# Token mixer of a hybrid block: attention products paired over halves of the array, decay rows broadcast by the tile loads

## The chip, the cores and the metric

The kernel runs on one core of a Trainium2 chip. The core has engines that run side by side and meet at semaphores: TensorE (PE in the rows, with PEld for the loads of its stationary operand), VectorE (DVE), ScalarE (ACT), GpSimd (POOL), and SyncE (SP), which here only starts DMAs. The metric is the time of one execution in device microseconds (us); smaller is better.

## The reference

One layer of an encoder block on 1024 tokens of width 1024, all in float32. The change touches the token mixer alone:

```python
def token_mixer(x, w_in, conv_w, a_log, dt_bias, norm_w, sinks, w_out):
    proj = x @ w_in
    ...
    gdn = gated_deltanet(qkv, z, b_raw, a_raw, conv_w, a_log, dt_bias, norm_w)
    swa = sliding_window_sink_attention(sq, sk, sv, sinks)
    return jnp.concatenate([gdn, swa], axis=-1) @ w_out
# gated_deltanet: 4 heads of 128, per chunk
    gam = cumsum(g);  decay = exp(gam_i - gam_j)
    a_mat = beta * strict_decay * (k @ k.T);  qk = (q @ k.T) * decay
    solve (I + a_mat) u = beta * v - beta * exp(gam) * k @ state
    o = q * exp(gam) @ state + qk @ u;  state = exp(gam_end) * state + k_dec.T @ u
# sliding_window_sink_attention: 8 query heads of 64, 2 key heads, window of 128
    s = q @ k.T / 8;  m = max(max(s), sink);  p = exp(s - m)
    p = p / (sum(p) + exp(sink - m));  o = p @ v
```

After it come a layer norm (x1), the PEER feed-forward (product-key retrieval over 16384 experts, 8 heads, top 16), and a second layer norm. Most of the kernel's time lies there, and the change leaves it as it is.

## The kernel before

`build` runs stages one after another: `project` (the input projection, to about 302 us), `mix_tokens` (the mixer, to about 785 us), then `split_x1`, `retrieve`, `index_picks`, `build_gates` and `experts`. A stage begins when all engines have left the one before.

`mix_tokens` works through 8 tiles of 128 tokens. Each engine has its own program, in an order written out by hand; the semaphores in `S` tie them together. A tile's work on PE, in `body(c, i, s, before, after)`:

- transposes of k and v (L594, L596), and the attention scores of half the heads (`scores(s, 0)`, L536: four products with 64 rows of contraction and 256 columns; the first call uses rows 0 to 63 of the array, `scores(s, 1)` rows 64 to 127);
- six levels (LV = 6, n = 0 to 5) that invert the triangular matrix by doubling. A level is L613 (the product x), then filler, then a wait for VectorE's masked copy `xs` (L923, semaphore `lm`), then L633 (skipped in the last level) and L636. VectorE adds their results to `tu[0]` (L930, semaphore `la`) and `tu[1]` (L938, semaphore `lb`);
- the filler in a level: a share (2, 2, 2, 2, 3, 3 and, after the levels, 2) of the output projection of the tile before (`project_out`, L530, three products of 512 columns for each share), the transposes of the probabilities of heads 0 to 3 (n = 2, L543), the scores of the other half (n = 3), and the steps of `ahead`, which prepare the next tile's decay matrices;
- after the levels: L642, L651 (the solution u, copied by ScalarE in L770), L657, L659, L660, the transposes of the other probabilities (L543), the values (L672: 16 products, pT stationary, 64 columns of v moving), the transposes of og (L677) and of the attention output on (L681). ScalarE copies the two results into `mixT` hi (L782, L784), VectorE takes the low parts (L989). The next tile's scores wait for the low part of the attention half, its projection for both.

`ahead` for tile d: VectorE spreads the decay sums over 128 columns (gB, L839), adds the causal mask to the keys' part (e0, L841), PE turns gB into rows that stand on every partition, four products for the k part (L552) and four for the q part (L557), both into PSUM bank 1; VectorE adds e0 to each (L845, L848, into `dm`), ScalarE takes the exponentials (eg, L738, and dm, L740). The products of keys with keys (L563) and with queries (L569) follow in the same bank, and VectorE multiplies them by dm (L855, L858).

The softmax of a half: VectorE scales and masks the scores (`softmax_scores`, L871), takes the maxima (`softmax_max`, L879 to L884), ScalarE the exponentials (L720, four calls of 128x256 with their sums, and L723), PE transposes, ScalarE copies to pT (`evacuate_probs`, L727). The division by the sum is done on the output (L968, L970, L981).

SP loads each tile's operands (`load`, five DMAs on L462, and `load_x`) for two tiles at the start, later for tile c + 2 as soon as tile c has released them. The w_out rows come in eight loads (L487), which tile 0 splits into high and low parts.

## Time and profile before

| | us |
|---|---|
| runs: median of 3 (lowest, highest) | 3359.24 (3352.19, 3367.15) |
| the profiled execution | 3360.03 |
| its span in the trace | 3358.4 |
| PE busy over the span | 2814.9 |
| VectorE busy | 2310.0 |
| ScalarE busy | 932.6 |
| GpSimd busy | 1587.4 |

The time is the span and 1.6 us around it. Stages do not overlap, so a microsecond that the mixer's last engine gains or loses is one of the kernel's time. A busy share over the whole span says nothing of a stage; the mixer's own rows are below. The profile's chain of waits begins at 1609 us and says nothing of the mixer, so its chain is followed in the instructions in order of time.

### The profile page before, as it was taken

To read this page: it belongs to the slowest core of one execution; us is meant where nothing else is said; L and a number is where in the kernel's file an instruction comes from. 1 tells how busy PE (TensorE), PEld (TensorE's weight loads), DVE (VectorE), ACT (ScalarE), POOL (GpSimd) and SP (SyncE) were. 2 spreads that over 40 slices of the span, in tenths; PEclk is the share of its full clock that TensorE was granted. 3 is DMA by queue.
4 is the path that set the end of the run, shared out by engine and by line. 5 is a ranking of instruction groups with operands and counts; after the bars stand their busy time and mean duration, and the time that the engine had idled before them with its cause. 6 is when DMAs were issued, how large, how long until landed. Compare 5 with 4: busy or idle time off the path is not lost.

```text
span 3358.4 us, 39617 instructions
## 1 busy us (share of the span) xinstructions
PE 2814.9 (84%) x14408; PEld 2187.2 (65%) x14408; DVE 2310.0 (69%) x4936; ACT 932.6 (28%) x1295; POOL 1587.4 (47%) x1196
## 2 busy tenths in 40 slices
PE   7996799996988546564466999999999999999996
PEld 6896788885766446553244667676667776766664
DVE  4511666651899989996576777777877777775445
ACT  4311322321444434342111222222222222222221
POOL 0000000101577755553666664666665667653543
PEclk9987899997988777877788999999999999999998
DMA  3323211202211059998999998999999999997984
GB/s 129 106 71 97 71 44 56 66 13 102 71 48 35 32 180 305 302 303 232 404 393 387 388 390 328 397 394 386 377 385 342 401 381 391 391 355 280 343 331 175
DMA packets 383433, 829.65 MB, mean 247 GB/s; under 512 B 158080, under 2 KB 180992, under 8 KB 383264
## 3 DMA queue, kind: packets, MB, share of 16 engines
q0 software_dynamic: 150864, 548.60, 42.7%
q1 hardware_dynamic: 232400, 278.84, 24.8%
q8 instruction: 100, 1.64, 0.2%
q14 instruction: 69, 0.57, 0.0%
HBM read 768.49 MB, written 58.85 MB: 246 GB/s over the span
## 4 chain that ended last, share of the span: by engine, by line
PE 15%; DMA 13%; POOL 12%; DVE 8%; issue 4%; ACT 0%; POOLq 0%; DVEq 0%; ACTq 0%
DMA e_u_row<-in_u,id_u 11%; POOL hold L1775 8%; POOL e_u_row L1766 4%; DVE e_u_row L1979 3%; PE psum L1837 3%; PE psum L1802 2%; PE psum L1823 2%; PE psum L1803 2%; PE psum L1804 2%; PE psum L1824 2%; PE psum L1825 2%; DMA hold<-in_v,id_v 2%; DVE e_y L1970 1%; DVE e_ul L1937 1%; DVE e_vl L1941 1%
## 5 line engine op out<-in xcount | busy, mean ns | idle before, releaser
L1775 POOL DMA_INDIRECT hold<-in_v,id_v x512 | 577.3, 1128 | 316.2 <-PE psum L1837 172.8
L1979 DVE CUSTOM_DVE_ANT_0 e_u_row<-e_u_row,hold 128x1024 f32<-128x1024 f32 x384 | 467.9, 1223 | 280.7 <-DMA e_u_row<-in_u,id_u 249.9
L1766 POOL DMA_INDIRECT e_u_row<-in_u,id_u x384 | 482.9, 1257 | 372.5 <-DVE hidden_s L1979 241.3
L1823 PE MATMUL psum<-e_vh,e_ah 128*128 128x512 f32 x1024 | 425.1, 415 | 114.2 <-DVE e_y L1970 83.1
L1824 PE MATMUL psum<-e_vl,e_ah 128*128 128x512 f32 x1024 | 412.3, 403 | 0.0
L1825 PE MATMUL psum<-e_vh,e_al 128*128 128x512 f32 x1024 | 410.1, 400 | 0.0
L1970 DVE TENSOR_TENSOR e_y<-e_y,psum 128x512 f32<-128x512 f32 x504 | 327.7, 681 | 82.7 <-PE psum L1825 57.3
L1823 PEld LDWEIGHTS psum<-e_vh,e_ah 128*128 128x128 f32 x1024 | 199.9, 195 | 230.3 <-DVE e_y L1970 103.3
L1802 PE MATMUL psum<-x1d_hi,e_uh 128*128 128x512 f32 x864 | 342.7, 397 | 0.0
L1803 PE MATMUL psum<-x1d_lo,e_uh 128*128 128x512 f32 x864 | 337.5, 391 | 0.0
L1804 PE MATMUL psum<-x1d_hi,e_ul 128*128 128x512 f32 x864 | 336.4, 389 | 0.0
L1533 PE MATMUL psum<-g_one,g_two 128*128 128x128 f32 x1024 | 176.9, 353 | 148.6 <-issue 133.2
L1837 PE MATMUL psum<-hold,e_column 128*32 128x512 f32 x2048 | 249.5, 605 | 34.3 <-DMA hold<-in_v,id_v 27.5
L1533 PEld LDWEIGHTS psum<-g_one,g_two 128*128 128x128 f32 x1024 | 171.8, 266 | 161.5 <-issue 161.5
L1588 POOL DMA_INDIRECT hold<-in_u,id_u x128 | 197.7, 1544 | 165.0 <-DVE hidden_s L1562 135.0
L1882 ACT ACTIVATE e_a<-psum 128x512 f32<-128x512 f32 x108 | 64.4, 596 | 621.7 <-PE psum L1804 456.2
L1004 POOL TENSOR_TENSOR m_h<-m_h,m_lng 128x1024 f32<-128x1024 f32 x8 | 18.8, 2352 | 451.1 <-DVE m_h L905 451.1
L1825 PEld LDWEIGHTS psum<-e_vh,e_al 128*128 128x128 f32 x1024 | 199.7, 195 | 45.0
L1824 PEld LDWEIGHTS psum<-e_vl,e_ah 128*128 128x128 f32 x1024 | 200.8, 196 | 39.5
L1871 ACT ACTIVATE e_vh<-e_vr 128x1024 fp32r<-128x1024 f32 x128 | 135.2, 1056 | 302.2 <-DMA e_vr<-in_v 276.1
L1802 PEld LDWEIGHTS psum<-x1d_hi,e_uh 128*128 128x128 f32 x864 | 162.1, 188 | 75.0 <-issue 41.9
L1603 ACT ACTIVATE g_tile<-psum 128x512 f32<-128x512 f32 x128 | 131.6, 1089 | 216.8 <-PE psum L1533 213.6
(319 smaller groups left out, 5534.0 us busy)
## 6 DMA issues: line engine op xcount, KB each, us to landing
e_vr<-in_v SPq DMA_DIRECT2D x128, 512.0 KB
e_ur<-in_uT SPq DMA_DIRECT2D x108, 512.0 KB
s_G<-g_tile SPq DMA_DIRECT2D x8, 4096.0 KB, 29.6
e_g<-s_G SPq DMA_DIRECT2D x128, 256.0 KB
p_wr<-in_w_ch SPq DMA_DIRECT2D x17, 512.0 KB, 3.8
s_ch<-p_out POOLq DMA_DIRECT2D x16, 512.0 KB, 3.8
m_ch<-s_ch SPq DMA_DIRECT2D x8, 1024.0 KB, 5.9
r_w<-in_wq SPq DMA_DIRECT2D x16, 512.0 KB
```

What stands on the lines that cost most here:

```text
L1533: last = nc.tensor.matmul(psum[:, n // 4, (n % 4) * NK:(n % 4 + 1) * NK], one2[s][:, n, :], one1[s][:, n, :], start=True, stop=True)
L1766: pool.indirect_dma_start(out=u_ring[n % U_RING][:], out_offset=None, in_=io["u"], in_offset=bass.IndirectOffsetOnAxis(ap=id_u[:, s, k:k + ...
L1775: pool.indirect_dma_start(out=v_ring[m % V_RING], out_offset=None, in_=io["v"], in_offset=bass.IndirectOffsetOnAxis(ap=id_v[:, t:t + 1], a ...
L1802: nc.tensor.matmul(psum[:, j, :], uh[j][:, k, :], x1d[0][:, k, :], start=(k == 0), stop=False)
L1803: nc.tensor.matmul(psum[:, j, :], uh[j][:, k, :], x1d[1][:, k, :], start=False, stop=False)
L1804: last = nc.tensor.matmul(psum[:, j, :], ul[j][:, k, :], x1d[0][:, k, :], start=False, stop=(k == KC - 1))
L1823: nc.tensor.matmul(acc, ah[s][j][:, r], vh[s][j][:, c], start=(j == 0), stop=False)
L1824: nc.tensor.matmul(acc, ah[s][j][:, r], vl[s][j][:, c], start=False, stop=False)
L1825: last = nc.tensor.matmul(acc, al[s][j][:, r], vh[s][j][:, c], start=False, stop=(j == 1))
L1837: last = nc.tensor.matmul(psum[32 * j:32 * j + 32, 6 + c, :], column[:, 32 * (4 * (n % Z_RING) + j) + 31 - i:32 * (4 * (n % Z_RING) + j) + ...
L1970: add = nc.vector.tensor_tensor(y[:, t, c], y[:, t, c], psum[:, 2 + q % 4, :], ALU.add)
L1979: nc.vector.tensor_tensor_reduce(row, row, xs[:, s, :], 1.0, 0.0, ALU.mult, ALU.add, hs[:, s, k:k + 1]).then_inc(dotted, 1)
```

## The change

Three parts, joined:

1. **Decay rows by DMA.** The sums of all tiles are transposed once (64x128), copied to `rowT`, stored to a tensor in HBM, and each tile's rows are loaded broadcast over 128 partitions (`rowB`, 512 KB a tile). gB, L552 and L557 go. VectorE and ScalarE read the rows from SBUF.
2. **Scores with alternating row halves.** A half of the heads is now two query blocks times both key heads: the four products of a call alternate between rows 0 to 63 (to PSUM bank 4) and rows 64 to 127 (to bank 5). The host reorders the sinks and the rows of w_out to match.
3. **Stationary values.** v (64 columns) is stationary and pT (128 columns) moves; the two key heads go to column halves 0 and 64 of the array. The output comes out transposed, so L681, `on` and its copy go. Since the queries now lie along the columns, the probabilities are divided beforehand: ScalarE scales each head's 128x256 (`scale_probs`, four calls a half, semaphore `p_nrm`), for which VectorE adds and inverts the sums a half at a time (`softmax_sum`).

Around these: the first transposes of probabilities move from n = 2 to n = 3, the second scores from n = 3 to n = 4, the second maxima from n = 4 to n = 5, and at the tile's end the attention half of `mixT` goes first.

```diff
+                sp.wait_ge(prep["rowT"], 1)
+                sp.dma_start(scr["rows"].rearrange("c (n t) -> (c n) t", t=P), rowT[:]).then_inc(prep["stored"], 16)
+                sp.wait_ge(prep["stored"], 16)
+                for s in range(2):
+                    load_rows(sp, s, s)
                 for k in range(KC):
...
                     load(sp, c + 2, s)
+                    load_rows(sp, c + 2, s)
...
                 def scores(s, half):
-                    for n in range(4):
-                        last = nc.tensor.matmul(ATT[:, n * 2 * P:(n + 1) * 2 * P],
-                                                ch[s][64 * half:64 * half + 64, N_CONV + n, :],
-                                                kw[s][64 * half:64 * half + 64, :], start=True, stop=True)
+                    for m in range(2):
+                        for r in range(2):
+                            rows_r = slice(AD * r, AD * r + AD)
+                            last = nc.tensor.matmul(psum[:, 4 + r, m * 2 * P:(m + 1) * 2 * P],
+                                                    ch[s][rows_r, N_CONV + 2 * half + m, :],
+                                                    kw[s][rows_r, :], start=True, stop=True)
...
-                        if n == 2:
-                            pe.wait_ge(S["prob"], 2 * c + 1)
+                        if n == 3:
+                            pe.wait_ge(S["p_nrm"], 2 * c + 1)
                             transpose_probs(0)
-                        if n == 3:
+                        if n == 4:
                             pe.wait_ge(S["p_ev"], 2 * c + 1)
                             scores(s, 1)
-                        if after and n in (0, 1, 2, 4):
-                            ahead(c + 1, i + s, 1 - s, min(n, 3))
+                        if after and n in (2, 4):
+                            ahead(c + 1, i + s, 1 - s, 2 if n == 2 else 3)
...
-                    for a in range(AH):
-                        r = a // 4
+                    for p in range(4):
                         for k in range(2):
-                            last = nc.tensor.matmul(psum[:, 4, a * AD:(a + 1) * AD], pT[:, a, k, :],
-                                                    vw[s][:, k, r * AD:(r + 1) * AD], start=(k == 0), stop=(k == 1))
+                            for r in range(2):
+                                last = nc.tensor.matmul(psum[AD * r:AD * r + AD, 4, p * P:(p + 1) * P],
+                                                        vw[s][:, k, AD * r:AD * r + AD],
+                                                        pT[:, 4 * (p // 2) + 2 * r + p % 2, k, :], start=(k == 0), stop=(k == 1),
+                                                        tile_position=(0, AD * r))
...
+                def scale_probs(c, half):
+                    act.wait_ge(S["rec"], 2 * c + half + 1)
+                    for a in range(4 * half, 4 * half + 4):
+                        last = nc.scalar.activation(sc[:, a, :], sc[:, a, :], ACT.Copy, scale=mx[:, 3, a:a + 1])
+                    last.then_inc(S["p_nrm"], 1)
...
                     nc.scalar.activation(uu[:], bank(1), ACT.Copy).then_inc(S["u_ev"], 1)
+                    scale_probs(c, 1)
                     act.wait_ge(S["ods"], now)
...
-                        dve.wait_ge(S["row_a"], d + 1)
+                        dve.wait_ge(tile_in[s][6], 16 * (i + 1))
                         dve.wait_ge(S["e0"], d + 1)
-                        nc.vector.tensor_tensor(dm[:, 0], bank(1), e_heads, ALU.add).then_inc(S["add_a"], 1)
+                        nc.vector.tensor_tensor(dm[:, 0], rowB[s][:, 0], e_heads, ALU.add).then_inc(S["add_a"], 1)
```

Where the instructions stand, on three places. PE at the end of a tile and the beginning of the next one (m_pT holds the transposed probabilities, m_vw the values). Before:

```order
L584 MATMUL psum<-cst,m_tu 128x128 x4
L672 MATMUL psum<-m_vw,m_pT 128x64 x16
L677 MATMUL psum<-cst,m_og 128x128 x4
L681 MATMUL psum<-cst,m_on 128x128 x4
L594 MATMUL psum<-cst,m_ch 128x128 x4
L596 MATMUL psum<-cst,m_ch 128x128 x4
L536 MATMUL psum<-m_kw,m_ch 128x256 x4
L613 MATMUL psum<-m_tu,m_aq 128x128 x4
```

After:

```order
L588 MATMUL psum<-cst,m_tu 128x128 x4
L676 MATMUL psum<-m_pT,m_vw 64x128 x16
L683 MATMUL psum<-cst,m_og 128x128 x4
L598 MATMUL psum<-cst,m_ch 128x128 x4
L600 MATMUL psum<-cst,m_ch 128x128 x4
L551 MATMUL psum<-m_kw,m_ch 128x256 x4
L617 MATMUL psum<-m_tu,m_aq 128x128 x4
```

The values have changed their operands, and the transposes of m_on are gone.

VectorE in levels 0 and 1 of tile 0 (later tiles have the same order). Before:

```order
L923 TENSOR_TENSOR m_xs<-psum,mats 128x512
L839 COPY m_gB<-m_rows 128x1024
L841 TENSOR_TENSOR m_e<-mats,m_nkey 128x512
L930 TENSOR_TENSOR m_tu<-m_tu,psum 128x512
L938 TENSOR_TENSOR m_tu<-m_tu,psum 128x512
L879 TENSOR_REDUCE m_mx<-m_sc 128x4
L881 TENSOR_TENSOR m_mx<-m_mx,m_sinks 128x4
L883 TENSOR_TENSOR m_mx<-m_sinks,m_mx 128x4
L884 TENSOR_SCALAR m_mx<-m_mx 128x4
L845 TENSOR_TENSOR m_dm<-psum,m_e 128x512
L923 TENSOR_TENSOR m_xs<-psum,mats 128x512
```

After:

```order
L939 TENSOR_TENSOR m_xs<-psum,mats 128x512
L849 TENSOR_TENSOR m_e<-mats,m_nkey 128x512
L946 TENSOR_TENSOR m_tu<-m_tu,psum 128x512
L953 TENSOR_TENSOR m_tu<-m_tu,psum 128x512
L887 TENSOR_REDUCE m_mx<-m_sc 128x4
L889 TENSOR_TENSOR m_mx<-m_mx,m_sinks 128x4
L891 TENSOR_TENSOR m_mx<-m_sinks,m_mx 128x4
L892 TENSOR_SCALAR m_mx<-m_mx 128x4
L853 TENSOR_TENSOR m_dm<-m_rowB,m_e 128x512
L939 TENSOR_TENSOR m_xs<-psum,mats 128x512
```

Only the copy to m_gB is gone; what stands between the add to m_tu and the next m_xs is the same.

VectorE in levels 4 and 5 of tile 0 (m_wout_lo is split in tile 0 alone; later tiles have the rest in this order). Before:

```order
L923 TENSOR_TENSOR m_xs<-psum,mats 128x512
L930 TENSOR_TENSOR m_tu<-m_tu,psum 128x512
L879 TENSOR_REDUCE m_mx<-m_sc 128x4
L881 TENSOR_TENSOR m_mx<-m_mx,m_sinks 128x4
L883 TENSOR_TENSOR m_mx<-m_sinks,m_mx 128x4
L884 TENSOR_SCALAR m_mx<-m_mx 128x4
L938 TENSOR_TENSOR m_tu<-m_tu,psum 128x512
L858 TENSOR_TENSOR m_aq<-psum,m_dm 128x512
L910 TENSOR_TENSOR m_wout_lo<-m_wout_raw,m_wout_hi 128x1024
L923 TENSOR_TENSOR m_xs<-psum,mats 128x512
L935 TENSOR_TENSOR m_faded<-m_state,m_decay 128x512
L938 TENSOR_TENSOR m_tu<-m_tu,psum 128x512
```

After:

```order
L946 TENSOR_TENSOR m_tu<-m_tu,psum 128x512
L953 TENSOR_TENSOR m_tu<-m_tu,psum 128x512
L879 SCALAR_TENSOR_TENSOR m_sc<-psum,m_wm 128x1024
L866 TENSOR_TENSOR m_aq<-psum,m_dm 128x512
L926 TENSOR_TENSOR m_wout_lo<-m_wout_raw,m_wout_hi 128x1024
L939 TENSOR_TENSOR m_xs<-psum,mats 128x512
L887 TENSOR_REDUCE m_mx<-m_sc 128x4
L889 TENSOR_TENSOR m_mx<-m_mx,m_sinks 128x4
L891 TENSOR_TENSOR m_mx<-m_sinks,m_mx 128x4
L892 TENSOR_SCALAR m_mx<-m_mx 128x4
L950 TENSOR_TENSOR m_faded<-m_state,m_decay 128x512
L953 TENSOR_TENSOR m_tu<-m_tu,psum 128x512
```

The second scores (L871, now L879) came from level 3 to level 4, and the second maxima from level 4 to the last level, behind its m_xs.

## Rows read from the trace of the kernel before

**Rows 1.** Busy time by stretch: us, busy (x) per engine, granted clock, DMA share, GB/s

```profile
333.00:385.00 52.00, 35.25 (x219) 31.62 (x219) 32.05 (x47) 15.40 (x30) 0.00 (x0) 0.83 0.25 80
...
500.00:552.30 52.30, 49.08 (x344) 42.96 (x344) 33.72 (x61) 14.03 (x32) 4.73 (x2) 1.00 0.17 53
```

**Rows 2.** Order of time, tile 3, levels 0 and 1: start, us, engine, line [idle before]

```profile
504.36 1.16 PE L613 MATMUL psum<-m_tu,m_aq 128*128 128x128 f32 x8
...
507.94 1.06 PE L633 MATMUL psum<-m_xs,m_tu 128*128 128x128 f32 x8
...
510.53 1.21 DVE L879 TENSOR_REDUCE m_mx<-m_sc 128x4 f32<-128x1024 f32 x1
...
512.75 0.68 DVE L923 TENSOR_TENSOR m_xs<-psum,mats 128x512 f32<-128x512 f32 x1
512.76 0.49 ACT L720 ACTIVATE m_sc<-m_sc,m_mx 128x256 f32<-128x256 f32 x1
...
513.88 1.06 PE L633 MATMUL psum<-m_xs,m_tu 128*128 128x128 f32 x8
```

**Rows 3.** Order of time, tile 3, levels 1 to 5 and L651

```profile
515.72 1.16 PE L613 MATMUL psum<-m_tu,m_aq 128*128 128x128 f32 x8
...
518.10 1.03 PE L543 MATMUL psum<-cst,m_sc 128*128 128x128 f32 x8
...
518.97 1.06 PE L563 MATMUL psum<-m_ch 128*128 128x128 f32 x8
...
519.87 1.06 PE L633 MATMUL psum<-m_xs,m_tu 128*128 128x128 f32 x8
...
524.19 1.99 PE L536 MATMUL psum<-m_kw,m_ch 64*128 64x256 f32 x8
...
526.11 1.16 PE L633 MATMUL psum<-m_xs,m_tu 128*128 128x128 f32 x8
...
531.99 1.06 PE L633 MATMUL psum<-m_xs,m_tu 128*128 128x128 f32 x8
...
537.22 1.16 PE L636 MATMUL psum<-m_tu,m_xs 128*128 128x128 f32 x8 [0.16 <-DVE m_xs L923]
...
541.06 1.13 PE L651 MATMUL psum<-m_vb,m_tu 128*128 128x128 f32 x8 [0.40 <-DVE m_vb L951]
```

**Rows 4.** Order of time, end of tile 3 and beginning of tile 4

```profile
547.81 3.79 PE L672 MATMUL psum<-m_vw,m_pT 128*128 128x64 f32 x32 [0.68 <-ACT m_pT L727]
...
549.61 1.13 DVE L976 SCALAR_TENSOR_TENSOR m_og<-psum,m_rms,m_zw 128x128 f32<-128x128 f32 x4
...
551.43 0.61 PE L677 MATMUL psum<-cst,m_og 128*128 128x128 f32 x4
...
554.65 1.96 PE L536 MATMUL psum<-m_kw,m_ch 64*128 64x256 f32 x8 [0.68 <-DVE m_mixT_lo L989]
...
556.54 0.97 PEld L613 LDWEIGHTS psum<-m_tu,m_aq 128*128 128x128 f32 x8 [0.33 <-issue]
```

**Rows 5.** Order of time, experts stage: eight products on four column quarters in turn

```profile
1757.55 1.92 PE L1837 MATMUL psum<-hold,e_column 128*32 128x512 f32 x16 [0.64 <-DMA hold<-in_v,id_v]
```

**Rows 6.** Order of time, tile 7, which has no step of ahead, levels 0 and 1

```profile
715.48 1.05 PE L633 MATMUL psum<-m_xs,m_tu 128*128 128x128 f32 x8
...
720.40 1.16 PE L633 MATMUL psum<-m_xs,m_tu 128*128 128x128 f32 x8 [0.54 <-DVE m_xs L923]
```

**Rows 7.** Order of time, the mixer's start (SPq: DMA issues of SP)

```profile
316.03 63.26 SPq L487 DMA_DIRECT2D m_wout_raw<-in_w_out  x8
...
317.89 0.69 DVE L845 TENSOR_TENSOR m_dm<-psum,m_e 128x512 f32<-128x512 f32 x1 [1.63 <-PE psum L552]
```

**Rows 8.** DMA issues of the page: KB each, us from issue to landing

```profile
p_wr<-in_w_ch SPq DMA_DIRECT2D x17, 512.0 KB, 3.8
```

**Rows 9.** Busy time by stretch, the mixer's start, columns as in Rows 1

```profile
306.00:322.00 16.00, 5.19 (x20) 4.49 (x20) 5.09 (x20) 6.21 (x14) 0.00 (x0) 0.50 1.05 326
```

**Rows 10.** Busy time by stretch, the projection stage, columns as in Rows 1

```profile
0.00:100.00 100.00, 81.70 (x342) 65.41 (x343) 46.72 (x43) 46.13 (x44) 4.72 (x12) 1.00 0.38 129
```

95 lines of the change are left out of this document (45 added, 50 removed).

## Prediction

> **What bounds the kernel now.** The stages do not overlap, and only the mixer changes. I read the busy times by stretch first: in one whole tile PE is busy for 49.1 of 52.3 us at the full granted clock (1.00, which is the 2.4 GHz level), VectorE for 33.7, ScalarE for 14.0 [rows 1]. So PE bounds a steady tile, but with little margin in places: the instructions in order of time show where PE waits for VectorE's m_xs or m_vb [rows 2, 3]. Then I followed tile 3 from its L613 of level 0 to that of tile 4, 504.36 to 556.54, 52.18 us [rows 2, 4]. The same order holds in tiles 1 to 6. Since every group's cost on PE follows from differences of start times, I lay the new order out with them.
>
> Costs on PE, by differences of starts. L633 and L636 together hold it for 1.84 (513.88 to 515.72), L613 and a projection share of two for 2.38 (to 518.10), the eight transposes for 0.87 (to 518.97), a group of four products such as L563 for 0.90 (to 519.87) [rows 2, 3]. Level 3 to 4 has L633, L636, L613, a share of three and L569: 5.88 less 1.84 and 0.90 leaves 3.1 for L613 with a share of three. Level 2 to 3 has L633, L636, L613, a share of two and the scores: 6.24 less 1.84 and 2.38 leaves 2.02 for a call of scores [rows 3]. Of that 0.33 is the idle time at its end [rows 4], so 1.7 is the stream of its 8 passes of 256 columns, 0.21 each. The values take 3.6 (L672 at 547.81, L677 at 551.43) [rows 4]. On VectorE an instruction over 512 columns takes 0.68 (m_xs, L923) and follows its forerunner at 0.6, or at 0.7 where it needs its result; over 1024 columns it takes 1.21 (L879) [rows 2], and I use that for the scores' mask too.
>
> **The sum for a steady tile, place by place (start of one named instruction to the next).**
>
> Level 0 (L613 to L633). Before 3.58 [rows 2]. PE no longer has L552, which leaves 2.38. But VectorE's order is vb, the scores' mask (1.2), m_xs (0.68), and since the scores come earlier (below) it is the late one: m_xs ends at about +2.6. Now 2.63.
>
> Level 0 to 1 (L633 to L633). Before 5.94 (507.94 to 513.88) [rows 2]. L557 leaves, 0.89. VectorE, though, runs without a gap from the add to m_tu through the maxima and the dm add (from 510.53, 1.6 + 0.6 us) to m_xs (512.75, ends 513.43). That stays, so PE waits: m_xs is ready at +5.5. Now 5.55, a gain of 0.4 only. Tile 7 bears this out: without any step of ahead its interval is 4.92 and PE waited 0.54 for m_xs [rows 6]; one add of 0.6 more makes 5.5.
>
> Level 1 to 2. Before 5.99 (to 519.87) [rows 2, 3]. The transposes leave for the next level, L563 stays: 1.84 + 2.38 + 0.90 = 5.1. VectorE (two m_tu adds, dm add, the new small softmax_sum of 0.4, m_xs) ends at +4.25: covered.
>
> Level 2 to 3. Before 6.24 (to 526.11) [rows 3]. The scores leave, the transposes come: 1.84 + 2.38 + 0.87 = 5.1. The transposes now wait for scale_probs. ScalarE does eg, dm, then four scalings. A call of 128x256 took 0.49 with its sum [rows 2]; at 0.5 each they end about 2.8 us before PE asks. Cost nothing; if one took 1.2 instead, the cover is gone.
>
> Level 3 to 4. Before 5.88 (to 531.99) [rows 3]. The scores come in: 1.84 + 3.1 + scores + 0.90. The price of the scores is unknown, as no row shows two row halves in turn. **Bounds:** 2.02 if they do not overlap, 1.17 if the stream of 1.7 halves. The nearest row is L1837: eight float32 products of 512 columns, two passes each, on four column quarters in turn, took 1.92 us [rows 5]. By the scores' 0.21 us for a pass of 256 columns, 16 passes of 512 would need 6.8 in a row, so 3.5 ran side by side. I take 1.17. Now 7.0; at the other end 7.85.
>
> Level 4 to 5 (L633 to L636). Before 5.23 [rows 3]. On VectorE the mask of the scores (1.2) replaces the maxima (1.6); the path m_tu, mask, aq, m_xs ends at +5.1. Now 5.15; PE alone would need 4.9.
>
> L636 to L651. Before 3.84 [rows 3]. The maxima (1.6) now stand behind the last m_xs, before faded, m_tu, m_xs, m_vb. VectorE becomes late: 1.65 + 0.6 + 0.7 + 0.7 + 0.75 gives 4.4. A loss of 0.55. Queued behind on VectorE are softmax_sum (0.4), the layer norm and the next inverse, which have over 1 us of cover.
>
> L651 to the values. Before 6.75 (541.06 to 547.81) [rows 3, 4]. ScalarE gets four scalings, 2.0 us, in its 3.0 us of idle before og. Unchanged.
>
> Values to the next L613. Before 8.73 (547.81 to 556.54) [rows 4]. The values on two column halves: 3.6 if they do not overlap, 1.8 if they do; L1837 is the same kind of overlap and I take 1.8. The transposes of og then wait for VectorE: og ends at 550.74 [rows 4], so they run at 550.8 (0.44), and those of the next tile to 552.2. ScalarE copies the attention half at 550.1; VectorE finishes normalize (1024 columns and a reciprocal, 1.0) at 551.8 and its low part at 552.45, so the scores start at 552.55 and L613 at 553.6. Now 5.8: a gain of 2.9, of which only 0.3 hangs on the values' overlap.
>
> Sum: 2.63 + 5.55 + 5.1 + 5.1 + 7.0 + 5.15 + 4.4 + 6.75 + 5.8 = 47.5, against 52.2. **4.7 us a tile, times six: 28.2.** PE gives up L552 and L557 (1.8), the transposes of m_on (0.4), 1.7 of scores and 1.8 of values, 5.7 of work a tile; it also loses some waits, and gains others for VectorE.
>
> **Edges.** Tile 0's end gains like the others, 2.8. Tile 7: scores 0.85, end 2.9, less 0.55: 3.2. Tile 0's levels run at a granted clock of 0.83 and with waits for w_out [rows 1]; they gain at least the 2 us of a steady tile's levels, at most about 6; I take 3. The start costs: the rows must go to HBM and back. SP is free for the store at 316.0 [rows 7], while its queue of some 4.3 MB at 326 GB/s drains until about 319.5 [rows 9]. So stored at 320.3, and a 512 KB load takes 3.8 to land [rows 8]: rows at 324.4, while the first dm add ran at 317.89 [rows 7]. But L552, L557, L563 and the waits between them are gone from this chain: counted back from the end of the second aq at 327.9 through aq, four slow products, aq, exp and two adds, rows at 321.8 would lose nothing. Loss 3 (bounds 0 and 8). w_out's loads start 8 us later under a cover of 25. Tile 0's levels and the start cancel. In later tiles the 512 KB are asked for a whole tile ahead, at a DMA share of 0.17 [rows 1]: nothing.
>
> Total 28.2 + 2.8 + 3.2 = 34. The profiled execution took 3360.0, the median was 0.8 less: **3326 us.**
>
> The trace shows 0.33 us of idle on PE behind the scores, at the change to the full array [rows 4]. The Trainium skill, page TensorEngine Tiling (Array Packing), section Key Properties, says that a change of tiling mode drains TensorE; it speaks against the change, which puts two more such changes around the values of each tile. By that, 2 x 0.33 x 8 = 5 us more, 3331; by the rows both lie in waits that exist anyway (0.68 for m_pT ahead, 1.0 for og behind), and nothing is added. The same section says that tiles load and multiply in parallel; L1837 agrees for columns (3.5 of 4), and no row shows it for row halves.
>
> **Rivals.**
> *The row halves do not overlap.* For it: nothing shows it, and both halves give to the same columns of the array. Level 3 to 4 loses 0.85, level 0 only 0.45, since VectorE is late there. 1.3 x 6 + 1.7 = 9.5: 3335. If the values do not overlap either, 0.3 x 8 more: 3338.
> *Waits on VectorE or ScalarE eat half the gain.* Three places are already set by VectorE, and I counted semaphore hops tightly; 0.3 us more at each of nine places is 2.7 a tile: 3342 to 3347.
> *Slower: the clock falls.* PE's busy share drops from 94% to about 90%, with waits of 1.4 us in level 1 and 1.1 before L651. Tile 0 shows what it costs: busy 68%, clock 0.83 [rows 1]. At 0.83 the 43 us of PE work a tile would need 8.9 more, 62 in seven tiles: 3388. It decides from a mean clock under 0.89. Against it: the projection stage is busy 82% at 1.00 [rows 10].
> *More gain than counted:* tile 0 at 6 instead of 3, the start free: 3320, and with less idle between places 3315.
>
> **How the numbers follow.** Forecast (3319 to 3332) 0.54; row halves serial (3333 to 3339) 0.20; half the gain eaten (3340 to 3350) 0.12; more than counted (3308 to 3318) 0.09; clock or an unknown stall (over 3350) 0.05. A measurement can tell about 0.5%, 16.8 us, from no change, so faster means under 3342.4: all of the first, second and fourth and a part of the third, 0.86; same 0.11; slower 0.03 (the clock's case, which lies above 3376 only if it holds in most tiles). The range 3312 to 3344 leaves out half of the fourth case, most of the fifth and part of the third, and takes in both ends of the scores' price and of the start.
>
> **What would show it.** A tile's period of about 47 us; L617 of level 0 to L637 under 2.8; level 0 to 1 at 5.5 with PE waiting 1.4 for m_xs; the scores' group at 1.2 and the values' at 1.8; no wait of PE for ScalarE's m_sc at the transposes; granted clock 1.00 from tile 1 on; the first dm add at 324 to 325. Wrong if the clock is under 1 in tiles 1 to 6, if the scores take 2.0, or if scale_probs ends late.

## The result, and the profile after

| | us |
|---|---|
| changed kernel, median of 4 runs (lowest, highest) | 3315.69 (3315.04, 3317.66) |
| kernel before, median of 4 runs on the same chip | 3361.89 (3352.19, 3367.15) |
| ratio, 95% interval | 0.9859 (0.9843, 0.9875) |
| the profiled execution, its span | 3315.04, 3313.4 |
| PE, VectorE, ScalarE busy | 2766.4, 2303.7, 957.6 |

The change saves 46 us by the two medians, where 34 were forecast. (The median before moved by 2.7 us, from 3359.24 to 3361.89, when a fourth run came to it; against the forecast of 3326 the changed kernel is 10 us lower.) The first question is where in the program they were saved. The mixer ends where SP issues the first load of `t_x`: at 786.70 before, at 745.76 now, 40.9 us earlier. The remaining 4.1 us of the two profiled executions lie in later stages that the change doesn't touch; they turn out to be within chance (see the second run of this kernel below).

The order of time on PE in tile 3 of the changed kernel, which answers to [rows 2 to 4], without the projection's products: start, us, engine, line, shape, and in brackets the idle time before and what ended it.

```profile
486.85 1.16 PE L617 MATMUL psum<-m_tu,m_aq 128*128 128x128 f32 x8
...
489.44 1.16 PE L637 MATMUL psum<-m_xs,m_tu 128*128 128x128 f32 x8
...
495.25 1.16 PE L637 MATMUL psum<-m_xs,m_tu 128*128 128x128 f32 x8 [1.32 <-DVE m_xs L939]
...
500.47 1.06 PE L637 MATMUL psum<-m_xs,m_tu 128*128 128x128 f32 x8
...
504.69 1.03 PE L558 MATMUL psum<-cst,m_sc 128*128 128x128 f32 x8
505.56 1.06 PE L637 MATMUL psum<-m_xs,m_tu 128*128 128x128 f32 x8
...
510.54 1.14 PE L551 MATMUL psum<-m_kw,m_ch 64*128 64x256 f32 x8
511.60 1.16 PE L573 MATMUL psum<-m_ch 128*128 128x128 f32 x8
512.60 1.06 PE L637 MATMUL psum<-m_xs,m_tu 128*128 128x128 f32 x8
...
517.66 1.16 PE L640 MATMUL psum<-m_tu,m_xs 128*128 128x128 f32 x8
...
521.96 1.13 PE L655 MATMUL psum<-m_vb,m_tu 128*128 128x128 f32 x8 [0.86 <-DVE m_vb L968]
...
528.71 1.97 PE L676 MATMUL psum<-m_pT,m_vw 128*64 128x128 f32 x32 [0.68 <-ACT m_pT L736]
531.70 0.66 PE L683 MATMUL psum<-cst,m_og 128*128 128x128 f32 x4 [1.02 <-DVE m_og L991]
...
533.30 1.14 PE L551 MATMUL psum<-m_kw,m_ch 64*128 64x256 f32 x8
```

Read it by differences of starts, as the sum was made. The scores hold PE from 510.54 to L573 at 511.60, 1.06 us, where a call took 1.92 to 2.02 before [rows 3, 4]. The values take 1.97 instead of 3.79 (by the length of the row; counted to the next group's start they took about 3.6 before). Each transpose of the probabilities comes without a wait. The next tile's L617 starts at 534.37, so this tile took 47.52 us against 52.18; the six steady tiles average 47.41. The last columns of the next view (busy time by stretch: us, busy and count of PE, PEld, VectorE, ScalarE and GpSimd, granted clock, DMA share, GB/s) answer to [rows 1].

```profile
338.00:374.00 36.00, 24.50 (x183) 21.88 (x182) 28.80 (x47) 14.54 (x31) 0.00 (x0) 0.93 0.22 67
427.00:474.50 47.50, 43.09 (x324) 37.53 (x324) 33.10 (x61) 16.95 (x39) 4.75 (x2) 1.00 0.21 70
...
522.00:569.50 47.50, 43.31 (x326) 37.72 (x327) 33.30 (x62) 16.96 (x39) 4.76 (x2) 1.00 0.21 69
```

PE is busy 91% of a steady tile instead of 94%, and the granted clock stays at 1.00. The start of the mixer answers to [rows 7]:

```profile
316.22 0.55 SPq L489 DMA_DIRECT2D s_rows<-m_rowT  x1
...
321.36 0.80 SPq L465 DMA_DIRECT2D m_rowB<-s_rows  x2
...
325.26 0.69 DVE L853 TENSOR_TENSOR m_dm<-m_rowB,m_e 128x512 f32<-128x512 f32 x1 [7.36 <-DMA m_rowB<-s_rows]
```

The rows went to HBM in 5.1 us and back in 3.9, and the first dm addition started at 325.26 instead of 317.89. VectorE idled 7.36 us for it, but level 0 of tile 0 began only 2.57 us later (338.45, before 335.88).

### The profile page after: what moved, and what is told of

It is laid out like the page before. It is cut to its first block, busy times and chain, and to the rows that moved or that the text cites. A ratio compares the mean times of both kernels' runs of the same rounds, so it can differ in the third digit from the quotient of the medians.

```text
span 3313.4 us, 39366 instructions
## 1 busy us (share of the span) xinstructions
PE 2766.4 (83%) x14249; PEld 2138.5 (65%) x14249; DVE 2303.7 (70%) x4936; ACT 957.6 (29%) x1360; POOL 1582.5 (48%) x1196
## 4 chain that ended last, share of the span: by engine, by line
PE 18%; DMA 13%; POOL 9%; DVE 9%; issue 4%; ACT 0%; POOLq 0%; DVEq 0%
DMA e_u_row<-in_u,id_u 12%; POOL hold L1785 6%; DVE e_u_row L1989 4%; PE psum L1847 3%; POOL e_u_row L1776 3%; PE psum L1833 3%; PE psum L1812 3%; PE psum L1813 2%; PE psum L1814 2%; PE psum L1834 2%; PE psum L1835 2%; DVE e_y L1980 1%; DVE e_ul L1947 1%; DVE e_al L1967 1%; DVE e_vl L1951 1%
## 5 line engine op out<-in xcount | busy, mean ns | idle before, releaser
L1847 PE MATMUL psum<-hold,e_column 128*32 128x512 f32 x2048 | 250.1, 607 | 28.6 <-DMA hold<-in_v,id_v 22.8
```

The source lines that it names most:

```text
L1847: last = nc.tensor.matmul(psum[32 * j:32 * j + 32, 6 + c, :], column[:, 32 * (4 * (n % Z_RING) + j) + 31 - i:32 * (4 * (n % Z_RING) + j) + ...
```

## The experiments

Each is compared by the first `t_x` issue of its profiled execution, which leaves the later stages out. Where an execution started the mixer late (the load of `m_alog` was issued at 303.8 before, and between 302.1 and 305.4 in the others), the text says so and takes it off. "A tile" is the mean of the six steady ones.

### Each part alone

The broadcast of the rows alone, on the kernel before (attention, softmax and levels as before):

```diff
-                        nc.vector.tensor_tensor(dm[:, 0], bank(1), e_heads, ALU.add).then_inc(S["add_a"], 1)
+                        nc.vector.tensor_tensor(dm[:, 0], rowB[s][:, 0], e_heads, ALU.add).then_inc(S["add_a"], 1)
...
+                    load_rows(sp, c + 2, s)
```

> The kernel before with part 1 alone (decay rows by DMA; scores, values and the order of levels as before). If the steady-tile sum holds: level 0 loses L552 and its wait (1.1 us), level 0 to 1 only 0.4 since VectorE sets it, so 1.5 a tile in seven tiles, less 2.6 at the start: about 8 us less than before, 3353 to 3355. Rival, every product removed counts in full: 1.8 a tile, less 2.6: 3351. Rival, the round trip through HBM and the loads cost more than they give: 3362 or more.

Measured: 3353.96 us, the median of 10 runs (3345.58 to 3365.46), ratio 0.9977 (0.9964 to 0.9991). Its first `t_x` issue is at 781.1, 7.2 earlier than before once the 1.6 us of a later start are off. A tile takes 51.14 on the mean, but one of the six is an outlier: the end of tile 6 ran for a while at the lower level of TensorE's clock (of the row of busy times below, as in [rows 1], the third number from the right is the granted clock).

```profile
702.00:706.00 4.00, 4.00 (x19) 3.60 (x20) 2.27 (x5) 1.30 (x3) 0.93 (x1) 0.50 0.02 4
```

That tile took 52.71 us; the other five average 50.83, a gain of 1.35. The time of 3354 is what the steady-tile sum said, and the 1.35 is near its 1.5.

The attention alone, that is the changed kernel with gB, L552 and L557 back:

```diff
-                        nc.vector.tensor_tensor(dm[:, 0], rowB[s][:, 0], e_heads, ALU.add).then_inc(S["add_a"], 1)
+                        nc.vector.tensor_tensor(dm[:, 0], bank(1), e_heads, ALU.add).then_inc(S["add_a"], 1)
...
-                    load_rows(sp, c + 2, s)
```

> The changed kernel without part 1 (gB and its products on PE are back), so parts 2 and 3 and the shifted levels alone. If the parts add up: about 8 us more than the changed kernel, 3324, that is 38 less than before. Rival, the parts need each other (VectorE's copy to m_gB eats the room that the shorter scores made): 3330 or more.

Measured: 3326.93 us (3324.80 to 3332.26), ratio 0.9891 (0.9871 to 0.9912); first `t_x` issue 756.7, a tile 49.57. The time lies between the 3324 of parts that add up and the 3330 of parts that need each other.

The ratios of the parts multiply to 0.9868, within the interval of the whole. By the tile, though, the parts give 1.35 (without the outlier) and 2.61 us, 3.96 together, and the change gives 4.77. The missing 0.8 has a place. From L613 of level 0 to that of level 1 the kernel before took 5.42 us, the rows alone 4.21, the attention alone 6.63, both 4.53 or 4.31. With the attention alone, PE reaches the filler of level 0 sooner, and VectorE's chain that ends in gB is late:

```profile
490.01 1.16 PE L614 MATMUL psum<-m_tu,m_aq 128*128 128x128 f32 x8
...
493.81 1.16 PE L553 MATMUL psum<-cst,m_gB 128*128 128x128 f32 x8 [1.25 <-DVE m_gB L845]
```

```profile
492.47 1.28 DVE L845 COPY m_gB<-m_rows 128x1024 f32 x1
493.67 0.68 DVE L847 TENSOR_TENSOR m_e<-mats,m_nkey 128x512 f32<-128x512 f32 x1
```

These are rows of the attention alone, tile 3, first of PE and then of VectorE. PE stands 1.25 us in front of L553 until the copy of gB (492.47, 1.28 us) is done. The other part removes this copy. So each part is worth more when the other is there.

### Is it the order of the halves that shortens the scores?

The four products of a call in the order half, product instead of product, half. Two of one row half then stand in a row:

```diff
-                    for m in range(2):
-                        for r in range(2):
+                    for r in range(2):
+                        for m in range(2):
```

> The changed kernel with the four products of a call of scores in the order rows 0 to 63 twice, then rows 64 to 127 twice, instead of alternating. If the alternating halves overlap on the array: the group goes from 1.06 us back to about 1.9, levels 3 to 4 lose 0.85 a tile, level 0 about 0.4: 3325. Rival, the group is short for another reason (the banks, or loads that run ahead): 3316 and a group of 1.1.

Measured: 3318.19 us (3316.76 to 3320.68), ratio 0.9868 (0.9847 to 0.9889); first `t_x` issue 745.7, a tile 47.40. What I held to be needed, the alternation, is not. The scores of this kernel, level 4 of tile 3:

```profile
512.13 1.14 PE L551 MATMUL psum<-m_kw,m_ch 64*128 64x256 f32 x8
513.20 1.16 PE L573 MATMUL psum<-m_ch 128*128 128x128 f32 x8
```

1.07 us, as in the change. That left two explanations: two row halves overlap without being alternated, or the group is short for another reason, such as the two banks of the accumulator. The next kernel tells them apart. It keeps the change's order and banks but takes all four products from row half 0, so half of the scores are those of other heads:

```diff
-                            rows_r = slice(AD * r, AD * r + AD)
+                            rows_r = slice(0, AD)
```

> The changed kernel with all four products of a group of scores in row half 0 (stationary and moving both from partitions 0 to 63), written to banks 4 and 5 in the same alternation as in the change; so half of the scores are of other heads than they should be, and everything after them is the same work on other numbers. If two row halves working at once is what shortens the group, it is back at 1.9 to 2.1 us a group (passes one by one every 0.215 us), 0.9 us longer, twice a tile on TensorE's path: a tile of 49.1 to 49.3, the first t_x issue 759 to 761 instead of 745.76, 3329 to 3332. If the alternation of two banks of the accumulator is what shortens it, the group stays at 1.06 us, the tile at 47.4, the first t_x issue at 745 to 747.

Measured: 3334.04 us in one run; first `t_x` issue 763.4, a tile 48.92. The scores of level 4, tile 3:

```profile
521.16 1.99 PE L551 MATMUL psum<-m_kw,m_ch 64*128 64x256 f32 x8
523.08 1.16 PE L573 MATMUL psum<-m_ch 128*128 128x128 f32 x8
```

1.92 us, as before the change. So two row halves at work at once shorten the scores, and the alternation of banks by itself does not. Whether the two halves would still overlap if both wrote to one bank, no run shows. Its price per tile was 1.5 us, less than the 1.7 to 1.9 expected. The issue at 763.4 is above the 759 to 761 expected, and the time above its 3329 to 3332, since tile 0 began 2.1 us later and took 59.04 us against 53.36. The lower clock is a part of both. This is the granted clock around the start of tile 0, in this kernel and then in the change:

```profile
334.00:342.00 8.00, 7.94 (x27) 6.40 (x28) 2.52 (x4) 0.60 (x1) 0.00 (x0) 0.50 0.00 0
342.00:350.00 8.00, 6.09 (x27) 5.50 (x26) 4.71 (x9) 0.47 (x2) 0.00 (x0) 0.56 0.00 0
```

```profile
334.00:342.00 8.00, 7.16 (x41) 6.03 (x42) 4.06 (x6) 0.60 (x1) 0.00 (x0) 0.74 0.00 0
342.00:350.00 8.00, 5.47 (x45) 5.00 (x43) 6.23 (x14) 4.14 (x12) 0.00 (x0) 1.00 0.01 2
```

The first scores took 3.78 us there (1.87 in the change), and level 0 to 1 took 6.43 (3.94). So what this one run says of row halves is read from the steady tiles.

### The same question for the values

First all eight products of one column half and then those of the other:

```diff
-                    for p in range(4):
-                        for k in range(2):
-                            for r in range(2):
+                    for r in range(2):
+                        for p in range(4):
+                            for k in range(2):
```

> The changed kernel with all values of the first key head (column half 0) before those of the second, so that neighbours on PE use the same half. If halves overlap only when they alternate: the group goes from 1.9 us to about 3.5, but only 0.3 a tile shows, since the wait for m_og (1.0 us idle before L683) covers the rest: 3318. Rival, all of it shows: 1.6 in eight tiles, 3329.

Measured: 3319.54 us (3314.53 to 3328.22), ratio 0.9866 (0.9843 to 0.9889); first `t_x` issue 747.7, a tile 47.65. Then two of one half in a row, and two of the other:

```diff
                     for p in range(4):
-                        for k in range(2):
-                            for r in range(2):
+                        for r in range(2):
+                            for k in range(2):
```

> The changed kernel with the 16 products of the values in the order pair, half, block: two products of one column half in a row, then two of the other, instead of turn by turn. With eight in a row the group took 3.33 us instead of 1.97 and no passes overlapped. If TensorE looks a few instructions ahead and starts the other half's product while this half's is still running, two in a row overlap as the four scores did: 1.9 to 2.2 us. If column halves overlap only where the program alternates them: 3.2 to 3.5 us, or, where only each change of half overlaps, 2.5 to 2.9. In each case the tile is little changed (the og transposes wait for VectorE then anyway): the first t_x issue 745 to 748.

Measured: 3327.74 us in one run; first `t_x` issue 749.6, of which 1.6 are a later start, a tile 47.39. (The expectation for the column halves and the one for the tile both held. The time of this single run is high through stages behind the mixer, see below.) The values in tile 3, first of the eight in a row, then of the pairs:

```profile
531.10 3.33 PE L676 MATMUL psum<-m_pT,m_vw 128*64 128x128 f32 x32 [0.68 <-ACT m_pT L736]
534.36 0.66 PE L683 MATMUL psum<-cst,m_og 128*128 128x128 f32 x4
```

```profile
531.41 2.02 PE L676 MATMUL psum<-m_pT,m_vw 128*64 128x128 f32 x32 [0.68 <-ACT m_pT L736]
534.39 0.66 PE L683 MATMUL psum<-cst,m_og 128*128 128x128 f32 x4 [0.97 <-DVE m_og L991]
```

Eight in a row take 3.33 us, two in a row 2.02, turn by turn 1.97. How far apart two halves may stand is in the same trace. The trace has two passes for each float32 product, 32 for the group. Cut at two moments, the eight in a row of tile 3 are

```profile
531.10 1.63 PE L676 MATMUL psum<-m_pT,m_vw 128*64 128x128 f32 x13 [0.68 <-ACT m_pT L736]
531.10 2.02 PE L676 MATMUL psum<-m_pT,m_vw 128*64 128x128 f32 x20 [0.68 <-ACT m_pT L736]
```

Thirteen passes have started by 532.465, seven more by 532.85, and the last twelve by 534.16. Pass by pass, the starts lie 0.11 us apart (only the first gap is 0.16) up to the twelfth and from the 21st on, and in between two such series run side by side: the last four passes of the one half with the first four of the other. All eight tiles have this pattern. So in this group PE brings the other half forward by four passes, two products, and not more, which is what both kernels with two of one half in a row need. (The trace doesn't name the half of a pass; that is read from the two series.) And the 1.36 us that eight in a row cost the group cost the tile only 0.24: before L683, PE waits for VectorE's `m_og` anyway (1.02 idle in the change, 0.97 with the pairs, none with eight in a row). That is the cover that the prediction put at all but 0.3.

No kernel separates the rest of part 3. From the values to the next L617 a steady tile gained 3.07 us (8.73 to 5.66), the largest gain of all places. With the scores in one row half this interval is 6.49, so 0.8 of it are the next tile's scores; the other 2.2 belong to the stationary values, the transposes that went with them and the attention half of `mixT` going first, together.

### Tile 0: what the shift by a level is worth

The largest miss was tile 0's levels: 7.2 us gained where 3 were put. I took the parts of the change alone there, and one more kernel, the kernel before with nothing but the shift (transposes in level 3, second scores in level 4, their mask and maxima one level later):

```diff
-                        if n == 2:
+                        if n == 3:
                             pe.wait_ge(S["prob"], 2 * c + 1)
                             transpose_probs(0)
-                        if n == 3:
+                        if n == 4:
                             pe.wait_ge(S["p_ev"], 2 * c + 1)
                             scores(s, 1)
```

> The kernel before with only the level shift of the attention: transposes of the first probabilities in level 3 instead of 2, second scores and their mask and maxima one level later. Nothing else of the change. What is measured is how much of tile 0's 7.2 us comes from the shift. My theory: in tile 0 the second scores stood at level 3 behind a pT copy that ScalarE made late, among the copies of w_out (PE idle 1.68 us there at 356.85), and the shift takes that wait away: L613 to L651 of tile 0 goes from 41.97 us to 37 to 39, steady tiles (52.17 us each) move by no more than 0.3, the first t_x issue comes at 781 to 786 instead of 786.70, and the time is 3355 to 3362. Rival 1: the shift by itself does nothing in tile 0 (41 to 42 us there), and the 5.4 us that the attention part gave tile 0 came from shorter groups and fewer instructions: no change, 3360 to 3364. Rival 2: the shift also carries much of the steady gain: a tile of 51.2 or less, the first t_x issue by 778, 3352 or less.

Measured: 3361.75 us, the median of 10 runs (3353.77 to 3371.90), ratio 1.0001 (0.9985 to 1.0017); first `t_x` issue 785.1, of which 1.6 are a later start, a tile 52.47. In the time the shift by itself makes no difference that can be measured: in the trace, tile 0 gains 3.3 us and each steady tile loses 0.3, both as expected. Tile 0 of five kernels, from one level's start to the next, in us:

| tile 0 | before | shift | rows | attention | both (after) |
|---|---|---|---|---|---|
| level 0 to 1 | 5.42 | 5.42 | 3.92 | 5.44 | 3.94 |
| level 1 to 2 | 7.50 | 7.49 | 6.20 | 5.92 | 5.63 |
| level 2 to 3 | 5.21 | 5.22 | 5.51 | 5.42 | 5.43 |
| level 3 to 4 | 8.25 | 5.16 | 9.11 | 5.17 | 5.17 |
| level 4 to 5 | 5.75 | 5.85 | 5.79 | 4.98 | 4.99 |
| level 5 to the u product | 9.84 | 9.67 | 8.93 | 9.68 | 9.61 |
| sum | 41.97 | 38.81 | 39.46 | 36.61 | 34.77 |

3.1 of the 7.2 us are the shift's, all between levels 3 and 4; 3.35 come from levels 0 to 2; 0.8 from the shorter scores in level 4. What stood there, tile 0 of the kernel before:

```profile
338.47 1.16 PE L552 MATMUL psum<-cst,m_gB 128*128 128x128 f32 x8 [1.43 <-DVE m_gB L839]
...
344.39 1.67 PE L557 MATMUL psum<-cst,m_gB 128*128 128x128 f32 x8 [1.93 <-DVE m_dm L845]
...
356.85 2.18 PE L536 MATMUL psum<-m_kw,m_ch 64*128 64x256 f32 x8 [1.68 <-ACT m_pT L727]
358.97 2.08 PE L633 MATMUL psum<-m_xs,m_tu 128*128 128x128 f32 x8
...
366.07 1.16 PE L633 MATMUL psum<-m_xs,m_tu 128*128 128x128 f32 x8 [1.86 <-DVE m_xs L923]
```

It is tempting to read the gain off these waits, but others stand in their places. The same two levels of the changed kernel, 1 and 3:

```profile
346.08 1.16 PE L637 MATMUL psum<-m_xs,m_tu 128*128 128x128 f32 x8 [2.53 <-DVE m_xs L939]
...
356.68 1.16 PE L637 MATMUL psum<-m_xs,m_tu 128*128 128x128 f32 x8 [1.19 <-DVE m_xs L939]
```

Over levels 0 to 4, PE's waits fall only from 7.4 to 6.0 us. The larger part is what PE has to do and how fast. L552 and L557 are gone, which held PE for 0.99 and 1.46 us. The second scores, 2.1 us, stood in level 3 behind ScalarE's copy to pT, which came late among the copies of w_out; one level later the copy is long done, and the scores fill time in which PE waited 1.86 for `m_xs`. And the kernel before ran twice at the lower of the clock's two levels (granted clock 0.62 and 0.69, as a mean of the stretch):

```profile
344.50:349.00 4.50, 4.50 (x26) 4.50 (x27) 1.12 (x3) 2.87 (x9) 0.00 (x0) 0.62 0.02 4
...
356.50:362.00 5.50, 5.15 (x22) 4.45 (x23) 1.38 (x3) 1.36 (x2) 0.00 (x0) 0.69 0.30 95
```

L633 and L636 took 2.95 us in the first (345.85 to 348.80) and 3.29 in the second (358.97 to 362.26), where 1.84 is usual: 2.6 us in all. In the changed kernel the granted clock is 1.00 from 342 to 360. Level 1 to 2 of the attention alone shows how much this is: it has L557's counterpart and the same wait of 1.93 ahead of it, its clock stays at 1.00, and it takes 5.92 us instead of 7.50. Why the clock fell in one kernel and not in the other, no run shows: PE's wait in level 1 alone doesn't decide it, since the change waits 2.53 us there and stays at 1.00. With the shift alone the first slow stretch is still there and the second is gone.

### VectorE's order, and tile 0 once more

After the change PE waits for VectorE at two places of a tile, 1.32 us in level 1 and 0.86 ahead of L655. In this kernel the dm addition of the k part goes from level 0 to level 1, the second mask ahead of the m_tu update of level 4, the second maxima to the end of level 4, and the second aq product from level 4 to level 5:

```diff
+                        if n == 4:
+                            softmax_scores(c, s, 1)
                         if n < LV - 1:
...
                         if n == 5:
-                            softmax_max(c, 1)
+                            if after:
+                                ahead(c + 1, i + s, 1 - s, 5)
...
                         if n == 4:
-                            softmax_scores(c, s, 1)
-                        if after and n in (0, 1, 2, 4):
-                            ahead(c + 1, i + s, 1 - s, {0: 1, 1: 2, 2: 4, 4: 5}[n])
+                            softmax_max(c, 1)
+                        if after and n == 1:
+                            ahead(c + 1, i + s, 1 - s, 1)
+                        if after and n in (1, 2):
+                            ahead(c + 1, i + s, 1 - s, {1: 2, 2: 4}[n])
```

> The changed kernel with VectorE's work in another order: the first dm addition for the next tile at level 1 instead of 0, the second mask ahead of the update of tu in level 4, the second maxima at the end of level 4, the second aq product after the mask of level 5. No work is added or left out. My theory: after the change TensorE waits for VectorE at two places of each tile, 1.32 us for m_xs in level 1 and 0.86 us for m_vb ahead of the u product; with these additions out of the way both shrink, 1.2 to 1.9 us less a tile of 47.4, the first t_x issue 10 to 15 us before 745.76, the time 3301 to 3306. Rival: the wait goes from one level to the next, since VectorE's whole work of a tile is what sets these levels: a tile of 47.0 to 47.6, the time 3312 to 3318. Second rival: the moved additions delay the masks or tu in level 1 or 5, which are waited for at once: a tile over 47.8, 3319 or more.

Measured: 3310.14 us (3307.66 to 3320.21), ratio 0.9843 (0.9825 to 0.9862); first `t_x` issue 739.7. A tile takes 46.08, 1.33 less, within what was expected. The waits of tile 3:

```profile
495.32 1.16 PE L637 MATMUL psum<-m_xs,m_tu 128*128 128x128 f32 x8 [0.62 <-DVE m_xs L939]
...
521.48 1.13 PE L655 MATMUL psum<-m_vb,m_tu 128*128 128x128 f32 x8 [0.40 <-DVE m_vb L973]
```

But the time lies between the two cases expected (3301 to 3306, or 3312 to 3318), and the mixer gained only 6 us of the expected 10 to 15, since tile 0 took 57.05 us instead of 53.36. To see whether that was the order's doing or chance, the changed kernel itself ran again beside three others on one chip:

> The changed kernel itself once more, unchanged, for two numbers: how much its time varies, and whether the 4.1 us that its profiled run gained behind the mixer (from the first t_x issue to the end 2567.6 us, before 2571.7) belong to it. In the other eight kernels of this study the same unchanged stages took 2569.0 to 2578.9 us. If they vary by chance: this run's stretch lies anywhere in 2567 to 2579 us, the first t_x issue at 745 to 747, and the median of its runs at 3315 to 3321. If the change makes them faster: 2567 to 2568 again, and a median of 3314 to 3317.

Measured: 3321.74 us, the median of 4 runs (3314.98 to 3328.16), ratio 0.9878 (0.9854 to 0.9903); first `t_x` issue 746.7. Its levels are as in the first profile, but its tile 0 took 56.00 us. The place, on PE in the first profile, on PE in this one, and on ScalarE in this one:

```profile
379.60 2.08 PE L661 MATMUL psum<-m_uu,m_kd 128*128 128x128 f32 x8 [3.45 <-ACT m_uu L780]
```

```profile
381.47 2.08 PE L661 MATMUL psum<-m_uu,m_kd 128*128 128x128 f32 x8 [5.38 <-ACT m_uu L780]
```

```profile
379.88 1.06 ACT L757 ACTIVATE m_wout_hi<-m_wout_raw 128x1024 fp32r<-128x1024 f32 x1 [2.52 <-DMA m_wout_raw<-in_w_out]
380.84 0.58 ACT L780 ACTIVATE m_uu<-psum 128x512 f32<-128x512 f32 x1
```

PE waits for ScalarE's copy of uu, ScalarE's copy stands behind the last copy of w_out, and that waits for its load. So the end of tile 0 hangs on how long a load takes, and the same kernel differs by 2.6 us there: 1.9 in this wait and the rest in the products behind it, which ran at the lower clock for longer. Tile 7 varies too, in the other direction: from its values to the first `t_x` issue the first profile has 31.19 us and this one 29.58. Behind the mixer this execution took 2571.0 us, the first one 2567.6, the kernel before 2571.7. Over the fourteen executions profiled here that stretch lies between 2567.2 and 2578.9. So the 4.1 us behind the mixer are well within what chance does.

The next kernel takes that wait away: ScalarE's last two copies of w_out stand behind its copy of uu.

```diff
                         split_wout(5)
-                        split_wout(6)
-                        split_wout(7)
                     act.wait_ge(S["u_mm"], now)
                     nc.scalar.activation(uu[:], bank(1), ACT.Copy).then_inc(S["u_ev"], 1)
+                    if not before:
+                        split_wout(6)
                     scale_probs(c, 1)
+                    if not before:
+                        split_wout(7)
```

> The changed kernel with ScalarE's last two copies of w_out in tile 0 put behind its copy of uu (all other order unchanged). In tile 0 the copy of uu came at 378.97 because a w_out copy ahead of it waited for its load, while the u product had been ready about 3.6 us earlier. If the w_out copies are what is left of tile 0's excess: u product to values in tile 0 falls from 12.7 us to 8.5 to 9.5, and the first t_x issue comes at 741 to 743. Rival: the clock stays at 1.2 GHz longer, or VectorE's splitting of the last two blocks is late instead, and 1 us or less is left: 744.5 to 746.

Measured: 3312.26 us in one run; first `t_x` issue 743.4, of which 1.4 are a later start. From the u product to the values tile 0 takes 9.12 us instead of 12.71 and 15.36: the u product at 374.60 and the copy of uu right behind it.

```profile
376.71 0.60 ACT L778 ACTIVATE m_uu<-psum 128x512 f32<-128x512 f32 x1 [2.67 <-PE psum L655]
...
383.72 1.97 PE L676 MATMUL psum<-m_pT,m_vw 128*64 128x128 f32 x32 [0.68 <-ACT m_pT L736]
```

VectorE's order in tiles 1 to 7 only, with the change's order in tile 0 (`if before` at each moved instruction):

> The changed kernel with the order of the run vector_order on VectorE in tiles 1 to 7 alone, and its own order in tile 0. There a tile fell from 47.41 to 46.08 us, but tile 0 grew by 3.6 us. If tile 0's loss came from the order of its instructions among the w_out copies: the first t_x issue at 736.5 to 738.5 (745.76 less 6 times 1.33 and what tile 7 gives), 3306 to 3310. If it came from the clock, by chance of the run: 739 to 742, 3309 to 3313.

Measured: 3314.20 us (3307.64 to 3314.79), ratio 0.9848 (0.9828 to 0.9868); first `t_x` issue 740.5, of which 1.5 are a later start; a tile 46.08, tile 0 54.54. The issue, also without the later start (739.0), lies in the second case of the expectation (739 to 742), if at its edge; the time is above both cases (3306 to 3313). The rows still find a part for the first case. Of tile 0's 3.7 us with the order in every tile, 1.5 stood ahead of the u product (36.25 us against 34.77), and they are gone here (34.75). In the eight profiled executions that have the change's order in tile 0 up to there and scores on both halves, this one among them, the sum is 34.75 to 34.77, so the 1.5 belong to the order. They came by way of the clock: with VectorE's order in tile 0, L637 and L640 of level 1 took 3.46 us (345.41 to 348.87) where 1.84 is usual. The rest stood at the w_out load, where even one and the same kernel differs by 2.6, and can't be told from chance.

Both edits together:

> The two edits together: VectorE's order in tiles 1 to 7 and ScalarE's last two w_out copies behind the copy of uu. If they add up: the first t_x issue at 733 to 735, the time 3302 to 3308, some 12 us below the changed kernel and the fastest of this study. Rival: tile 0's gain is lost again at the start of tile 1, where the projection waits for VectorE's last w_out block: as vector_order_from_1 within 1 us.

Measured: 3307.46 us (3304.01 to 3309.99), ratio 0.9837 (0.9818 to 0.9855); first `t_x` issue 730.6, or 732.4 without its earlier start; tile 0 48.39, a tile 46.08. They add up. This is the fastest kernel of the study, 14 us below the changed kernel's four runs on the same chip and 8 below its first four.

## Why the prediction was right, and which term was off

The forecast was 3326 with a range of 3312 to 3344. The changed kernel's two medians are 3315.7 and 3321.7; both lie in it. The second is in the likeliest case (3319 to 3332); the first is 3 us below it, where the case "more gain than counted" stood (3308 to 3318), which names tile 0 at 6 instead of 3. The sum, place by place, in tile 3:

| place | before | predicted | measured |
|---|---|---|---|
| level 0 (L617 to L637) | 3.58 | 2.63 | 2.59 |
| level 0 to 1 | 5.94 | 5.55 | 5.81 |
| level 1 to 2 | 5.99 | 5.1 | 5.22 |
| level 2 to 3 | 6.24 | 5.1 | 5.09 |
| level 3 to 4 | 5.88 | 7.0 | 7.04 |
| level 4 to 5 | 5.23 | 5.15 | 5.06 |
| L640 to L655 | 3.84 | 4.4 | 4.30 |
| L655 to the values | 6.75 | 6.75 | 6.75 |
| values to the next L617 | 8.73 | 5.8 | 5.66 |

Six steady tiles gave 28.6 where 28.2 were put. That holds for the waits too: PE was to wait 1.4 for `m_xs` in level 1 and did for 1.32, and scale_probs, on which the transposes wait, was early. Tile 3 on ScalarE:

```profile
499.63 1.69 ACT L731 ACTIVATE m_sc<-m_sc,m_mx 128x256 f32<-128x256 f32 x4
```

The four scalings took 1.69 us instead of 2.0 and ended at 501.3, 3.4 before L558 at 504.69, where 2.8 were put.

**The price of the scores** was bounded by 1.17 and 2.02 and taken at 1.17, by the row of eight products on column quarters [rows 5]. The group took 1.06, and the kernel with one row half puts it back at 1.92. Counted as the sum counts it (level 3 to 4 less everything else in it) the price is 7.04 - 1.84 - 3.1 - 0.90 = 1.2, so the 1.17 was right for the sum. The rival with row halves in series is dead, and the bound it stood on was the right one: that kernel lost 1.5 a tile, where 1.3 was put. What I had wrong is the cause I named in testing it: that the halves must alternate.

**The change of tiling mode.** The Trainium skill, page TensorEngine Tiling (Array Packing), section Key Properties, says that such a change drains TensorE, and 5 us were put against it as a rival. The loads of the stationary operand show it around the scores (PEld, level 4 of tile 3):

```profile
510.54 0.73 PEld L551 LDWEIGHTS psum<-m_kw,m_ch 64*128 64x128 f32 x8 [0.35 <-issue]
511.60 0.97 PEld L573 LDWEIGHTS psum<-m_ch 128*128 128x128 f32 x8 [0.33 <-issue]
```

0.35 ahead and 0.33 behind, with nothing waited for; the kernel before has 0.37 and 0.33 there. So these rows agree with the page, and the price was there before. They are rows of the loads, though; the prediction calls the 0.33 us idle time on PE. With one half at work PE starts a pass of the scores every 0.215 us, so of the 1.92 us of a call before and of the 1.06 after (eight and four passes in a row) 0.2 us each are not passes: that is what PE itself loses in a call, not 0.33 at each end. Around the values, where the two changes are new, PE's wait ahead is 0.68 for m_pT as before [rows 4], the one behind is 1.02 for `m_og`, and the tile's end came to 5.66 where the sum without a drain had 5.8. There they cost nothing on the path.

**VectorE eats half the gain, or the clock falls:** neither. No place was over the sum by more than 0.26, and the clock was 1.00 in each steady tile at 91% busy. The first `dm` addition came at 325.26 (324 to 325 were put) and level 0 of tile 0 2.6 us later (3 were put).

**The term that was off** is "Tile 0's levels run at a granted clock of 0.83 and with waits for w_out [rows 1]; they gain at least the 2 us of a steady tile's levels, at most about 6; I take 3". They gained 7.2, in both executions. The term was read from an average over a stretch (clock 0.83, busy 68%) and not from rows of that stretch. Tile 0's own rows show what could go: the row products (0.99 and 1.46 us), the second scores of 2.1 us with a wait of 1.86 one level later that could take them in, and 2.6 us of slow L633 and L636. The first two could have been counted beforehand; that the clock would no longer fall there could not. The prediction had the clock as a rival in which the change makes it worse, and in tile 0's levels it got better. Of the "start loses 3, tile 0 gains 3" that cancelled, only the loss was right. Two smaller terms came out low in the first profile, and both are within chance: tile 0 from the u product on gave 3.6 where 2.8 were put, and 0.9 in the second execution; tile 7 gave 4.1 where 3.2 were put, and 5.7 in the second. The kernel before was profiled once, and its 34.73 us behind the values of tile 7 are 1.9 above the 32.86 and 32.76 of the rows alone and the shift alone, which have the same instructions there. So some 2 us of the mixer's gain can be this one execution's chance.

So the mixer gained 40.9 in the first profile and 40.0 in the second, against 34 predicted. (That the two agree so well is luck: the second lost 2.6 at the end of tile 0 and won 1.6 in tile 7.) Of the first profile's miss of 6.7, 4.2 is tile 0's levels, 0.9 tile 7, 0.8 the end of tile 0, and 0.4 each the six steady tiles and the start. The other 4 us of the first result are the unchanged stages. The forecast was right, then, by its steady tiles; what it missed in tile 0 and what chance added both went the same way, and still stayed within the range.

## What to carry to other kernels

Lay a change out place by place in one steady tile, with the start differences of named instructions; then do the same for the first and last tile from their own rows, since an average over a disturbed stretch hides what the change removes. Where a wait goes, look for the one that takes its place before you count it as gained. Float32 products that use half of the array's rows or columns should stand within two products of their partner on the other half: here two in a row overlapped in full, and of eight in a row only the last two. Two parts that shorten both ends of a handshake between engines are worth more together than one by one, so an experiment with each alone must be read by place and not only by total.
